# A hybrid attention and RG-LRU block on one Trainium2 core: weights packed in order of use, squares and sums of the inputs on other engines

## The chip, the cores and the metric

The kernel runs on 1 core of a Trainium2 chip. The metric is device time of one launch in microseconds (us). Three runs of the kernel before gave 1709.41, 1717.29 and 1715.06 us, median 1715.06. The engines are TensorE (PE; PEld is its weight loads), VectorE (DVE), ScalarE (ACT), GpSimd (POOL) and SyncE (SP), which here issues nearly all DMAs. A buffer in SBUF has 128 partitions (P).

## The reference

One layer, 256 tokens of width 2048, memory of 256 tokens, all in 32-bit floats:

```
h = rmsnorm(x, g_mix);  proj = h @ w_in        # q, k, v, forget, LRU x, LRU gate, memory q, merge gates
y_fox = forgetting_attention(q, k, v, log_f)   # 8 heads of 128
y_lru = rg_lru(conv4(lx)) * gelu(lg)           # width 1024
mk, mv = split(rmsnorm(mem, g_mem) @ w_mem_kv)
y_mem = memory_attention(qm, km, vm)           # 4 heads of 256
merged = sum(sigmoid(gate_logits + b_gate) * (branches @ w_branch))
x = x + merged @ w_out
up = conv3(rmsnorm(x, g_ffn) @ w_ffn_up);  x = x + (gelu(u_act) * u_val) @ w_ffn_down
```

`rmsnorm(x, g)` is `x * rsqrt(mean(x*x) + eps) * g`, the mean over the 2048 channels.

## The kernel before

All weights, 568 units of 512 x 256 floats (512 KB), stream through four slots. Channels lie on partitions and tokens along the free dimension; x and mem are each 16 tiles (kt) of 128 channels by 256 tokens. For precision each operand is held as a high part (rounded to fp32r) and the low rest, and three of the four products are computed: one matmul of 512 columns and one of 256, 16 matmuls a unit.

A unit u passes through these steps, all in order on their engines:

- SP `load` (L315 to L321) waits for lo_done of unit u-4 and fills slot u mod 4 of `raw`.
- ScalarE `split` (L585 to L593) waits for the weights and for TensorE to have finished unit u-4 (the wait for pe_units u-3), and copies `raw` to the high part of `W`.
- VectorE `split` (L894 to L898) subtracts, giving the low part, and counts up lo_done.
- TensorE `group` (L345 to L375) waits for lo_done of u and multiplies into `psG`; 4 units make a group, 256 output columns. When a group's last unit is u, ScalarE copies half of the sum (`copy_low`, L601) and VectorE adds the other (`add_low`, L904) ahead of their split of u+4.

Units 0 to 15 are phase mv (memory values, from XM = gained mem), 16 to 19 memory keys (XM), 20 to 23 memory queries (the first that read X, the normed and gained x), and so on. The root of mem is not in XM: it is applied later, to k by GpSimd (`scale_k`, L1360, when unit 19's group has been evacuated, about VectorE's unit 23) and to v by `rstd_tok`.

The start, in order of each engine:

- SP: all parameters (`par`, L325), then four times a mv unit and a chunk of four mem tiles (L328), then four times a chunk of x (L330) and a unit, then constants and `ff_raw` (L335), which takes 16 x 128 pieces of 32 bytes out of w_in.
- ScalarE: four times split(c) and four XM high tiles (`gained_hi`, L723); VectorE: four times split(c) and four XM low tiles (`gained_lo`, L1066). TensorE waits in its first group for every tile (memX_lo).
- From unit 4 on `run_units` calls split(u) and then `start_steps(u)` on ScalarE and on VectorE: parameters at 4, ff_w at 10, the lambda steps at 11 to 13, at unit 16 the roots and reciprocals (L718, L1119), at 18 to 21 the X high and low tiles of chunks 0 to 3.
- GpSimd (L1329 to L1353): squares of mem chunk by chunk, added up and folded to `sum1`, then the same of x; after the reciprocal, x_n = x * rstd in four products of 128x1024.
- TensorE adds over partitions by a matmul with ones (`channel_sums`, both inputs at once and the per-token column), as a hook after unit 12.

In the weight arrays a unit is 512 rows of 1 KB, each in its own row of w_in (49184 bytes apart), w_mem_kv and so on. xT and memT are 2048 rows of 1 KB.

Of the kernel before, what the change touches and what calls it, by code (L numbers as in the profile page):

```python
# [12 lines left out]
P = 128  # L34
# [43 lines left out]
for _name, _n in [("g_mix", KT), ("g_mem", KT), ("g_ffn", KT), ("b_gate", 3 * KT), ("w_fconv", 3 * 2 * FT),  # L78
                  ("b_fconv", 2 * FT), ("w_lconv", 4 * BT), ("b_lconv", BT), ("b_a", BT), ("b_x", BT),
                  ("lam", BT), ("g_q", 1), ("g_k", 1), ("g_qm", 2), ("g_km", 2), ("b_f", 1)]:  # L80
    PAR[_name] = _c
    _c += _n
# [54 lines left out]
def hybrid_layer_kernel(nc, xT, memT, par, shapes_const, w_in, w_mem_kv, w_rg, w_branch, w_out, w_up, w_down, outT):  # L137
    with ExitStack() as ctx:
# [22 lines left out]
        sq0 = sb("sq0", [P, UK, T], 112 * KB)  # L161
        sum0 = sb("sum0", [P, 2, UK, T], 116 * KB)
        sum1 = sb("sum1", [P, 2, T], 124 * KB)
# [82 lines left out]
        par_in, const_in, ff_in, rg_in = sem("par_in"), sem("const_in"), sem("ff_in"), sem("rg_in")  # L246
        setup, ones_set, pool_step = sem("setup"), sem("ones_set"), sem("pool_step")
        act_warm = sem("act_warm")
        sq_done, ss_done, rstd_done = sem("sq_done"), sem("ss_done"), sem("rstd_done")
# [26 lines left out]
        rows = lambda w: w.rearrange("(k p) c -> p k c", p=P)  # L276
        w_in_r, w_kv_r, w_br_r, w_out_r, w_up_r, w_down_r = map(rows, (w_in, w_mem_kv, w_branch, w_out, w_up, w_down))

        def unit_source(phase, i, k, q):

            if phase == "down":
                w, kk = k // (FT // UK), k % (FT // UK)
                return w_down_r[:, kk * UK:(kk + 1) * UK, bass.ds(i * (4 * UC) + w * UC, UC)]
            if phase == "branch0":
                return w_br_r[:, bass.ds(i * BT + (k % 2) * UK, UK), bass.ds(q * (2 * UC) + (k // 2) * UC, UC)]
            w, kk = k // 4, k % 4
            if phase == "gate0":
                src, col = w_in_r, i * D + q * (2 * UC) + (COL_GATE + w * UC)
            elif phase == "mv":
                src, col = w_kv_r, i * (2 * UC) + (BW + w * UC)  # L290
            elif phase == "mkq":
                src, col = (w_kv_r, i * UC) if w == 0 else (w_in_r, i * UC + COL_MQ)
            elif phase == "lru":
                src, col = w_in_r, i * UC + (COL_LX if w == 0 else COL_LG)
            elif phase == "v":
                src, col = w_in_r, i * (2 * UC) + (COL_V + w * UC)
            elif phase == "qk":
                src, col = w_in_r, i * UC + (COL_Q if w == 0 else COL_K)
            elif phase == "out":
                src, col = w_out_r, i * (2 * UC) + w * UC  # L300
            else:
                src, col = w_up_r, i * UC + w * FFN
            return src[:, kk * UK:(kk + 1) * UK, bass.ds(col, UC)]


# [9 lines left out]
        def _(sp):  # L315
            def load(phase, i, k, u, coef, before=0, q=0):

                s = u % SLOTS
                if i is not None or u >= SLOTS:
                    sp.wait_ge(lo_done, at(u - 3, i, coef) + before)  # L320
                sp.dma_start(raw[:, s], unit_source(phase, 0 if i is None else i, k, q)).then_inc(raw_full[s], 16)  # L321

            mem_r = memT.rearrange("(k p) t -> p k t", p=P)
            x_r = xT.rearrange("(k p) t -> p k t", p=P)
# [10 lines left out]
            sp.dma_start(ff_raw[:], w_in_r[:, :, COL_FF:COL_FF + 8]).then_inc(ff_in, 16)  # L335
            def load_phase(name, first=0, before=0, q=0):
                n, per = next((n, per) for ph, n, per in PHASES if ph == name)
                with sp.Fori(first, n) as i:
                    for k in range(NG[name] * per):
                        load(name, i, k, U0[name] + k, NG[name] * per, before, q)  # L340

            load_phase("mv", first=1)
            for name in ("mkq", "lru", "v", "qk"):
                load_phase(name)
            with sp.Fori(0, 4) as q:  # L345
                load_phase("gate0", before=q * QUARTER_UNITS, q=q)
                load_phase("branch0", before=q * QUARTER_UNITS, q=q)
            for name in ("out", "up", "down"):
                load_phase(name)
# [1117 lines left out]
```

## Time and profile before

| | |
|---|---|
| median of three runs | 1715.06 us |
| span of the profiled execution | 1705.0 us |
| TensorE busy, weight loads | 1670.0 us, 1445.4 us |
| VectorE, ScalarE, GpSimd busy | 1136.7, 888.3, 126.4 us |
| DMA | 306.34 MB, mean 180 GB/s, 307168 of 308044 packets under 2 KB |

A row of the order of time reads: start in us, duration in us, engine, line, operation, output <- inputs, shape, count; in brackets the idle time before it and what ended it. Rows of instructions by line give counts and durations in ns (min/median/max), first and last start in us. Rows by stretch give for each engine busy us and the count of instructions, then the granted TensorE clock (1.00 is 2.4 GHz, 0.50 is 1.2 GHz), the mean busy share of the DMA engines and GB/s. Busy time of TensorE is modelled at its ends; a change of the clock is known only from the first one on.

### The profile page before, as it was taken

Reading aid. Unit: us, or ns where it says so; the run is one execution under the profiler, and the core shown is the slowest. Engines: PE = TensorE matmul, PEld = TensorE weight load, DVE = VectorE, ACT = ScalarE, POOL = GpSimd, SP = SyncE. Lnnn points to the kernel's source line nnn. Section 1 sums busy time; section 2 is a strip of 40 time slices with the busy share of each in tenths; the row PEclk is TensorE's granted clock in tenths of the full one; section 3 lists DMA queues with packets and bytes.
Section 4 is the critical chain, followed back from the end, with each engine's and each line's share of the span. In section 5 each row is a group of like instructions: output and inputs, shape, how many; then the busy total and the mean of one; then the engine's idle time right before and its main releaser. Section 6 shows DMA issues by size and latency. Waiting matters only on the chain.

```text
span 1705.0 us, 27268 instructions
## 1 busy us (share of the span) xinstructions
PE 1670.0 (98%) x9386; PEld 1445.4 (85%) x9386; DVE 1136.7 (67%) x1302; ACT 888.3 (52%) x1135; POOL 126.4 (7%) x90
## 2 busy tenths in 40 slices
PE   4999999999999999999999999999999999999998
PEld 3778888887888888888888888888888888888887
DVE  8786667668765647466576677777777777644543
ACT  3466667555654545544545555555555555433342
POOL 7132212120000000000001000000000000000000
PEclk7899999999999999999999999999999999999999
DMA  6555557564555766657655656666555665666653
GB/s 211 161 161 160 145 157 204 161 173 136 150 155 183 191 185 180 189 183 187 184 186 184 189 168 197 197 188 193 183 186 185 196 192 184 197 204 198 203 191 110
DMA packets 308044, 306.34 MB, mean 180 GB/s; under 512 B 11744, under 2 KB 307168, under 8 KB 308000
## 3 DMA queue, kind: packets, MB, share of 16 engines
q1 hardware_dynamic: 307056, 302.89, 58.4%
q0 software_dynamic: 944, 2.88, 0.6%
q8 instruction: 25, 0.41, 0.1%
q14 instruction: 19, 0.16, 0.0%
HBM read 303.64 MB, written 2.10 MB: 179 GB/s over the span
## 4 chain that ended last, share of the span: by engine, by line
PE 95%; DVE 3%; DMA 1%; ACT 0%; POOL 0%; issue 0%; SPq 0%; ACTq 0%; DVEq 0%; POOLq 0%
PE psG L360 91%; PE psM L360 3%; DVE XM L1066 1%; DVE W L898 1%; DMA mem_raw<-memT 0%; DVE X L1066 0%; DMA lru_rg<-w_rg 0%; DVE rstd L1119 0%; POOL x_n L1353 0%; PE psM L448 0%; PE psM L446 0%; ACT X L723 0%; ACT L718 0%; ACT W L593 0%; POOL lru_rg L1386 0%
## 5 line engine op out<-in xcount | busy, mean ns | idle before, releaser
L360 PE MATMUL psG<-X,W 128*128 128x512 f32 (+1 forms) x5632 | 995.4, 338 | 0.0
L360 PEld LDWEIGHTS psG<-X,W 128*128 128x128 f32 x5632 | 862.1, 188 | 125.4 <-issue 3.4
L898 DVE TENSOR_TENSOR W<-raw,W 128x1024 fp32r<-128x1024 f32 x568 | 700.2, 1246 | 334.3 <-ACT W L593 331.8
L593 ACT ACTIVATE W<-raw 128x1024 fp32r<-128x1024 f32 x568 | 592.0, 1054 | 356.1 <-PE psG L360 349.5
L360 PE MATMUL psG<-hidden,W 128*128 128x512 f32 (+1 forms) x1408 | 244.2, 336 | 0.0
L360 PEld LDWEIGHTS psG<-hidden,W 128*128 128x128 f32 x1408 | 215.2, 188 | 28.9
L601 ACT ACTIVATE low<-psG 128x512 f32<-128x512 f32 x140 | 83.7, 598 | 239.1 <-PE psG L360 239.1
L360 PE MATMUL psG<-Y,W 128*128 x768 | 136.3, 340 | 0.0
L360 PEld LDWEIGHTS psG<-Y,W 128*128 128x128 f32 x768 | 117.7, 188 | 18.0
L1259 DVE SCALAR_TENSOR_TENSOR up_c<-up_pad,par_sb,up_c 128x256 f32<-128x256 f32 x176 | 77.5, 482 | 42.4 <-ACT up_c L842 36.4
L360 PE MATMUL psG<-merged,W 128*128 128x512 f32 (+1 forms) x512 | 90.6, 340 | 0.0
L360 PEld LDWEIGHTS psG<-merged,W 128*128 128x128 f32 x512 | 78.4, 188 | 12.1
L360 PE MATMUL psG<-W,XM 128*128 128x512 f32 (+1 forms) x256 | 59.9, 397 | 25.8 <-DVE XM L1066 25.2
L842 ACT ACTIVATE up_c<-up_pad,par_sb 128x256 f32<-128x256 f32 x88 | 48.2, 596 | 60.5 <-DVE up_pad L1251 60.5
L360 PEld LDWEIGHTS psG<-W,XM 128*128 128x128 f32 x256 | 47.2, 227 | 37.8 <-issue 21.5
L904 DVE TENSOR_TENSOR yd<-psG,low 128x512 f32<-128x512 f32 x40 | 27.7, 692 | 51.3 <-ACT low L601 51.3
L1426 POOL DMA_DIRECT2D outT<-xs x7 | 5.1, 734 | 696.7 <-DVE xs L1305 696.7
L360 PE MATMUL psG<-XM,W 128*128 128x512 f32 (+1 forms) x256 | 49.1, 350 | 3.1 <-DVE W L898 3.1
L360 PEld LDWEIGHTS psG<-XM,W 128*128 128x128 f32 x256 | 40.6, 194 | 10.5 <-DVE W L898 3.9
L904 DVE TENSOR_TENSOR up_pad<-psG,low 128x512 f32<-128x512 f32 x44 | 30.4, 692 | 27.7 <-ACT low L601 27.7
L866 ACT ACTIVATE hidden<-up_c 128x512 f32 (+1 forms) x22 | 13.9, 632 | 65.3 <-DVE up_c L1284 65.3
L360 PE MATMUL psG<-W,X 128*128 128x512 f32 (+1 forms) x256 | 45.4, 338 | 0.0
(181 smaller groups left out, 789.8 us busy)
## 6 DMA issues: line engine op xcount, KB each, us to landing
raw<-w_in SPq DMA_DIRECT2D x192, 512.0 KB, 4.1
raw<-w_up SPq DMA_DIRECT2D x176, 512.0 KB, 4.5
raw<-w_down SPq DMA_DIRECT2D x88, 512.0 KB, 3.5
raw<-w_branch SPq DMA_DIRECT2D x48, 512.0 KB, 3.4
raw<-w_mem_kv SPq DMA_DIRECT2D x32, 512.0 KB, 3.7
raw<-w_out SPq DMA_DIRECT2D x32, 512.0 KB, 4.2
mem_raw<-memT SPq DMA_DIRECT2D x4, 512.0 KB, 9.1
xs<-xT SPq DMA_DIRECT2D x4, 512.0 KB, 8.6
```

The source lines that it names most:

```text
L360: return nc.tensor.matmul(*a, skip_group_check=True, **kw)
L593: nc.scalar.activation(W[:, s, :, 0], raw[:, s], ACT.Copy).then_inc(hi_done, 1)
L601: nc.scalar.activation(low[:, g % 2], psG[:, b:b + 2, T:], ACT.Copy).then_inc(low_copied, 1)
L842: ins = nc.scalar.activation(up_c[w][:, t], up_pad[w][:, t, 2:], ACT.Identity, bias=p1("b_fconv", i * 2 + (w * FT + t)), scale=p1("w_fconv ...
L866: nc.scalar.activation(hidden[:, bass.ds(i * 2, 2), 0, :], up_c[1][:], ACT.Copy).then_inc(hidden_hi, 1)
L898: V.tensor_tensor(W[:, s, :, 1], raw[:, s], f32(W[:, s, :, 0]), ALU.subtract).then_inc(lo_done, 1)
L904: V.tensor_tensor(dst, psG[:, b:b + 2, 0:T], low[:, g % 2], ALU.add).then_inc(evac_done, 1)
L1066: ins = V.scalar_tensor_tensor(dst[:, k, 1, :], src[:, k], p1(gain, k), f32(dst[:, k, 0, :]), ALU.mult, ALU.subtract)
L1259: ins = V.scalar_tensor_tensor(up_c[w][:, t], up_pad[w][:, t, n:n + T], p1("w_fconv", i * 2 + (n * 2 * FT + w * FT + t)), up_c[w][:, t], A ...
L1426: G.dma_start(outT[bass.ds(i * UC, UC), :].rearrange("(a p) t -> p a t", p=P), xs[:, bass.ds(i * 2, 2)]).then_inc(out_stored, 16)
```

## The change

- All weights come as one array `w_units` [568, 128, 1024], the units in their order of use, each partition's 4 KB in one piece; SP's loads from unit 8 on are one loop. xT and memT are stored as [128, 16, 256], so a partition's four tiles of a chunk are 4 KB in one piece. `w_ff` is stored apart, one piece of 512 bytes per partition.
- SP first loads the 16 columns of g_mem (`gain_in`); then mem chunk before weights; the rest of the parameters after the four pairs.
- ScalarE in the first four units does the XM tiles before the split. At units 4 to 7 it squares a chunk of x, at 10 to 13 a chunk of mem.
- VectorE adds the squares: for x at units 6, 8 and 9, for mem at 12, 14 and 15. It makes the reciprocal of x at unit 12, x_n at 13 to 16 and the X low tiles at 16 to 19 (ScalarE the high ones there too). The roots and reciprocals of mem come at unit 22.
- TensorE's hook is in two: `x_sums` after unit 8, `mem_sums` after unit 17.
- GpSimd's start is gone; it begins with `scale_k`.

```diff
-            sp.dma_start(par_sb[:], par).then_inc(par_in, 16)
+            sp.dma_start(par_sb[:, 0:KT], par[:, 0:KT]).then_inc(gain_in, 16)
             for c in range(4):
-                load("mv", None, c, c, 0)
-                sp.dma_start(mem_raw[:, 4 * c:4 * c + 4], mem_r[:, 4 * c:4 * c + 4]).then_inc(mem_in[c], 16)
+                sp.dma_start(mem_raw[:, 4 * c:4 * c + 4], memT[:, 4 * c:4 * c + 4]).then_inc(mem_in[c], 16)
+                load(c, c)
+            sp.dma_start(par_sb[:, KT:], par[:, KT:]).then_inc(par_in, 16)
             for c in range(4):
-                sp.dma_start(xs[:, 4 * c:4 * c + 4], x_r[:, 4 * c:4 * c + 4]).then_inc(x_in[c], 16)
-                load("mv", None, 4 + c, 4 + c, 0)
+                sp.dma_start(xs[:, 4 * c:4 * c + 4], xT[:, 4 * c:4 * c + 4]).then_inc(x_in[c], 16)
+                load(c, 4 + c, c + 1)
...
-            sp.dma_start(ff_raw[:], w_in_r[:, :, COL_FF:COL_FF + 8]).then_inc(ff_in, 16)
...
+            sp.dma_start(ff_raw[:], w_ff).then_inc(ff_in, 16)
+            with sp.Fori(2, U_ALL // SLOTS) as i:
+                for s in range(SLOTS):
+                    sp.wait_ge(lo_done, i * SLOTS + (s - 3))
+                    src = w_units[bass.ds(i * SLOTS + s, 1)].rearrange("a p (k c) -> p (a k) c", k=UK)
+                    sp.dma_start(raw[:, s], src).then_inc(raw_full[s], 16)
...
-            def channel_sums():
-
-                pe.wait_ge(sq_done, 2)
-                mm(psM[:, 0, :], ones[:], sum1.rearrange("p j t -> p (j t)"), start=True, stop=True)
+            def x_sums():
+                pe.wait_ge(sums_ready, 1)
+                mm(psM[:, 0, 0:T], ones[:], sum1[:, 0], start=True, stop=True).then_inc(ss_done, 1)
+
+            def mem_sums():
+                pe.wait_ge(sums_ready, 2)
+                mm(psM[:, 1, 0:T], ones[:], sum1[:, 1], start=True, stop=True)
...
-                    group("mv", i, w, m_op, {4: channel_sums}, rows_major=True)
+                    group("mv", i, w, m_op, {0: x_sums}, rows_major=True)
...
-            mkq(None, {})
+            mkq(None, {1: mem_sums})
...
             for c in range(4):
-                split(c)
                 act.wait_ge(mem_in[c], 16)
                 for k in range(4 * c, 4 * c + 4):
                     gained_hi(XM, mem_raw, "g_mem", (k,)).then_inc(memX_hi, 1)
+                split(c)
+            act.wait_ge(par_in, 16)
 
             def start_steps(u):
+                if 4 <= u < 8:
+                    act.wait_ge(x_in[u - 4], 16)
+                    nc.scalar.activation(sq0[:, u - 4], xs[:, 4 * (u - 4):4 * (u - 4) + 4], ACT.Square).then_inc(sq_done, 1)
+                if 10 <= u < 14:
+                    act.wait_ge(sum_step, 4)
+                    act.wait_ge(sums_ready, 1)
+                    nc.scalar.activation(sq0[:, u - 10], mem_raw[:, 4 * (u - 10):4 * (u - 10) + 4], ACT.Square).then_inc(sq_done, 1)
...
-                if u == 16:
+                if u == 12:
                     act.wait_ge(ss_done, 1)
-                    root_mean_square(rstd0.rearrange("p j t -> p (j t)"), psM[:, 0, :])
-                    root_mean_square(rstd_tok[:], psM[:, 1, 0:2]).then_inc(root_done, 1)
-                if 18 <= u < 22:
-                    c = u - 18
+                    root_mean_square(rstd0[:, 1], psM[:, 0, 0:T]).then_inc(root_done, 1)
+                if u == 22:
+                    act.wait_ge(ss_done, 2)
+                    root_mean_square(rstd0[:, 0], psM[:, 1, 0:T])
+                    root_mean_square(rstd_tok[:], psM[:, 2, 0:2]).then_inc(root_done, 1)
+                if 16 <= u < 20:
+                    c = u - 16
...
+                for first, j in ((6, 0), (12, 1)):
+                    if u == first:
+                        dve.wait_ge(sq_done, 4 * j + 2)
+                        V.tensor_tensor(sq0[:, 0], sq0[:, 0], sq0[:, 1], ALU.add).then_inc(sum_step, 1)
+                    if u == first + 2:
+                        dve.wait_ge(sq_done, 4 * j + 4)
+                        V.tensor_tensor(sq0[:, 2], sq0[:, 2], sq0[:, 3], ALU.add).then_inc(sum_step, 1)
+                        dve.wait_ge(sum_step, 4 * j + 2)
+                        V.tensor_tensor(sq0[:, 0], sq0[:, 0], sq0[:, 2], ALU.add).then_inc(sum_step, 1)
+                    if u == first + 3:
+                        dve.wait_ge(sum_step, 4 * j + 3)
+                        V.tensor_tensor(sq0[:, 0, 0:2], sq0[:, 0, 0:2], sq0[:, 0, 2:4], ALU.add).then_inc(sum_step, 1)
+                        dve.wait_ge(sum_step, 4 * j + 4)
+                        V.tensor_tensor(sum1[:, j], sq0[:, 0, 0], sq0[:, 0, 1], ALU.add).then_inc(sums_ready, 1)
...
-                if u == 16:
+                if u == 12:
                     dve.wait_ge(root_done, 1)
-                    V.reciprocal(rstd0[:], rstd0[:])
+                    V.reciprocal(rstd0[:, 1], rstd0[:, 1]).then_inc(rstd_done, 1)
+                if u == 22:
+                    dve.wait_ge(root_done, 2)
+                    V.reciprocal(rstd0[:, 0], rstd0[:, 0])
                     V.reciprocal(rstd_tok[:], rstd_tok[:]).then_inc(rstd_done, 1)
-                if 18 <= u < 22:
-                    c = u - 18
+                if 13 <= u < 17:
+                    c = u - 13
+                    dve.wait_ge(rstd_done, 1)
+                    V.tensor_tensor(x_n[:, 4 * c:4 * c + 4], xs[:, 4 * c:4 * c + 4],
+                                    rstd0[:, 1:2].to_broadcast([P, 4, T]), ALU.mult).then_inc(x_scaled, 1)
+                if 16 <= u < 20:
+                    c = u - 16
                     dve.wait_ge(xX_hi, c + 1)
...
-            pool.wait_ge(rstd_done, 1)
-            for c in range(4):
-                G.tensor_tensor(x_n[:, 4 * c:4 * c + 4], xs[:, 4 * c:4 * c + 4],
-                                rstd0[:, 1:2].to_broadcast([P, 4, T]), ALU.mult).then_inc(x_scaled, 1)
+            pool.wait_ge(rstd_done, 2)
```

## Rows read from the trace of the kernel before

**Rows 1.** The page: busy time of TensorE, and its busy tenths by slice.
```profile
PE 1670.0 (98%) x9386; PEld 1445.4 (85%) x9386; DVE 1136.7 (67%) x1302; ACT 888.3 (52%) x1135; POOL 126.4 (7%) x90
...
PE   4999999999999999999999999999999999999998
```

**Rows 2.** Busy time by stretch: all engines, clock, DMA share, GB/s.
```profile
12.00:49.00 37.00, 22.79 (x65) 15.48 (x65) 37.00 (x20) 10.91 (x19) 35.25 (x17) 0.66 0.51 154
36.00:49.00 13.00, 6.76 (x17) 4.37 (x18) 13.00 (x8) 1.06 (x3) 12.40 (x7) 0.56 0.30 66
80.00:100.00 20.00, 16.93 (x95) 14.50 (x95) 18.68 (x15) 13.40 (x25) 11.76 (x4) 0.97 0.33 84
```

**Rows 3.** Waits, the whole span: who waited for whom, us, times, longest.
```profile
PE psG L360 <- DVE XM L1066: 25.2, 11, 11.6
```

**Rows 4.** Order of time, the first 49 us.
```profile
5.30 1.06 ACT L593 ACTIVATE W<-raw 128x1024 fp32r<-128x1024 f32 x1 [2.94 <-DMA raw<-w_mem_kv]
...
9.18 1.70 ACT L723 ACTIVATE XM<-mem_raw,par_sb 128x256 fp32r<-128x256 f32 x4 [2.83 <-DMA mem_raw<-memT]
...
11.55 5.46 PE L360 MATMUL psG<-W,XM 128*128 128x512 f32 x16 [11.55 <-DVE XM L1066]
...
15.21 1.71 ACT L723 ACTIVATE XM<-mem_raw,par_sb 128x256 fp32r<-128x256 f32 x4 [0.35 <-DMA mem_raw<-memT]
...
18.23 1.71 ACT L723 ACTIVATE XM<-mem_raw,par_sb 128x256 fp32r<-128x256 f32 x4 [0.37 <-DMA mem_raw<-memT]
...
48.81 11.54 PE L360 MATMUL psG<-W,XM 128*128 128x512 f32 x49 [0.57 <-DVE W L898]
```

**Rows 5.** Instructions of L1066 and L898, count and ns min/median/max.
```profile
L1066 DVE SCALAR_TENSOR_TENSOR XM<-mem_raw,par_sb,XM x16: 474/2108/2595, 9.7 to 43.9; 128x256 fp32r<-128x256 f32 x16
L1066 DVE SCALAR_TENSOR_TENSOR X<-x_n,par_sb,X x16: 469/472/2640, 89.0 to 104.6; 128x256 fp32r<-128x256 f32 x16
...
L898 DVE TENSOR_TENSOR W<-raw,W x568: 1153/1225/3386, 6.4 to 1690.3; 128x1024 fp32r<-128x1024 f32 x190
```

**Rows 6.** Order of time, 60 to 106 us.
```profile
62.45 0.49 DVE L1093 TENSOR_TENSOR ff_w<-ff_raw,ff_w 128x128 fp32r<-128x128 f32 x2
...
66.10 0.17 DVE L1102 SCALAR_TENSOR_TENSOR lam_d<-lam_u,lam_m 128x8 f32<-128x8 f32 x1
...
66.94 1.28 ACT L749 ACT_TABLE_LOAD   x1
...
80.41 3.35 DVE L1119 RECIPROCAL rstd<-rstd 128x512 f32<-128x512 f32 x1 [0.93 <-ACT rstd_tok L718]
...
83.87 11.76 POOL L1353 TENSOR_TENSOR x_n<-xs,rstd 128x1024 f32<-128x1024 f32 x4 [34.53 <-DVE rstd_tok L1120]
...
96.22 0.68 DVE L904 TENSOR_TENSOR mem_v<-psG,low 128x512 f32<-128x512 f32 x1
...
97.96 1.66 DVE L1066 SCALAR_TENSOR_TENSOR X<-x_n,par_sb,X 128x256 fp32r<-128x256 f32 x4
...
98.09 4.62 PE L360 MATMUL psG<-XM,W 128*128 128x512 f32 x16 [3.06 <-DVE W L898]
...
102.55 11.26 PE L360 MATMUL psG<-X,W 128*128 128x512 f32 x64
```

**Rows 7.** DMA of 0 to 50 us: GB/s in 40 slices.
```profile
GB/s 0 61 354 320 301 317 342 386 353 347 349 347 350 350 347 348 348 320 91 34 0 0 0 239 350 243 7 0 0 0 29 317 242 84 10 4 0 0 0 25
```

**Rows 8.** TensorE in two stretches of 60 us: busy, clock, DMA share, GB/s.
```profile
500.00:560.00 60.00, 60.00 (x342) 1.00 0.61 181
980.00:1040.00 60.00, 60.00 (x349) 1.00 0.59 185
```

**Rows 9.** Three windows of 2 us, all engines, clock, DMA share, GB/s.
```profile
12.00:14.00 2.00, 2.00 (x7) 1.65 (x7) 2.00 (x3) 1.80 (x5) 1.75 (x1) 1.00 1.10 348
56.00:58.00 2.00, 2.00 (x13) 1.77 (x12) 0.71 (x1) 0.62 (x1) 0.00 (x0) 1.00 0.76 253
100.00:102.00 2.00, 2.00 (x8) 1.71 (x7) 2.00 (x5) 0.00 (x0) 0.00 (x0) 0.50 0.66 226
```

More of the change, by code:

```diff
@@ L134, in at, with hybrid_layer_kernel @@
     return const if i is None else i * coef + const
[L137 removed]
+def hybrid_layer_kernel(nc, xT, memT, par, shapes_const, w_units, w_ff, w_rg, outT):
     with ExitStack() as ctx:
@@ L274, in f32 @@
             return ap.bitcast(F32)
[L276 to L303, printed above, removed]
         QUARTER0, QUARTER_UNITS = U0["gate0"], U0["gate1"] - U0["gate0"]
@@ L334, in _ @@
             sp.dma_start(mask[:], shapes_const[:, P:P + CW]).then_inc(const_in, 16)
-            sp.dma_start(ff_raw[:], w_in_r[:, :, COL_FF:COL_FF + 8]).then_inc(ff_in, 16)
[L336 to L349, printed above, removed]
+            sp.dma_start(ff_raw[:], w_ff).then_inc(ff_in, 16)
[3 more added lines that the diff above has]
+                    src = w_units[bass.ds(i * SLOTS + s, 1)].rearrange("a p (k c) -> p (a k) c", k=UK)
+                    sp.dma_start(raw[:, s], src).then_inc(raw_full[s], 16)
             for t in (KT - 2, KT - 1):
@@ L1427, in _, with _unit, _unit_sources, _tokens_last @@
             pool.wait_ge(out_stored, 16 * (KT // 2 - 1))
+def _unit(w, sources):
+    src, row, col = sources
+    rows = w[src][row:row + UK * P, col:col + UC]
+    return rows.reshape(UK, P, UC).transpose(1, 0, 2).reshape(P, UK * UC)
+def _unit_sources():
+    for phase, i, w, last in GROUPS:
+        per = next(per for name, _, per in PHASES if name == phase)
+        q = int(phase[-1]) if phase[:-1] in ("gate", "branch") else 0
+        for k in range(per):
+            row = k * UK * P
+            if phase == "down":
+                yield "w_down", row, i * 4 * UC + w * UC
+            elif phase[:-1] == "branch":
+                yield "w_branch", i * BW + row, q * 2 * UC + w * UC
+            elif phase[:-1] == "gate":
+                yield "w_in", row, COL_GATE + i * D + q * 2 * UC + w * UC
+            elif phase == "mv":
+                yield "w_mem_kv", row, BW + i * 2 * UC + w * UC
+            elif phase == "mkq":
+                yield ("w_mem_kv", row, i * UC) if w == 0 else ("w_in", row, COL_MQ + i * UC)
+            elif phase == "lru":
+                yield "w_in", row, (COL_LX if w == 0 else COL_LG) + i * UC
+            elif phase == "v":
+                yield "w_in", row, COL_V + i * 2 * UC + w * UC
+            elif phase == "qk":
+                yield "w_in", row, (COL_Q if w == 0 else COL_K) + i * UC
+            elif phase == "out":
+                yield "w_out", row, i * 2 * UC + w * UC
+            else:
+                yield "w_up", row, i * UC + w * FFN
+def _tokens_last(x):
+    return np.ascontiguousarray(x.T.reshape(KT, P, T).transpose(1, 0, 2))
 def _columns(v):
```

64 lines of the change are left out of this document (22 added, 42 removed).

## The prediction

> **What bounds the kernel now.** I read the page first: TensorE is busy in 98% of the span, and its slice line shows 9 everywhere except in the first tenths [rows 1]. So only what shortens TensorE's idle or half-speed time can shorten the whole, and I went on to the table by stage. It shows where that time lies: from 12 to 49 us TensorE is busy 22.8 of 37 us at a mean granted clock of 0.66; a second, small hole lies at 80 to 100 us, 3.1 us of idle time [rows 2]. In the same 37 us VectorE is busy without a break and so, nearly, is GpSimd (35.25 us), while the DMA share has fallen to 0.30 by the end. The waits name whom TensorE waits for: 25.2 us for VectorE's XM [rows 3].
>
> The order of time shows the pace. First matmul at 11.55, first matmul of unit 4 at 48.81 [rows 4]: 37.26 us for four units. At full clock four units take 11.26 us (2.82 each), and the first unit took 5.46 [rows 4, 6]: it ran at 1.2 GHz, for 12 to 14 us hold 7 matmuls, like the 8 of a stretch granted 0.50 and unlike the 13 at 1.00; the clock column only shows no change there [rows 9]. VectorE is late because its instructions are stretched. An XM tile takes 474 ns at best and 2108 at the median, and the same instruction on X 472 at the median; a split W takes 1225 at the median and 3386 at worst [rows 5]. Four X tiles alone take 1.66 us, four XM tiles at the median 8.4 [rows 5, 6]. The long ones lie where GpSimd runs a tensor_tensor; that is the cause I take. ScalarE and the DMAs are not late: ScalarE's XM had been started by 18.23 at the latest, 30 us before unit 4 [rows 4].
>
> **The change part by part.** All is summed against the profiled span, 1705.0 us; the shown median, 1715.06, is 10.1 above it, and I carry that over.
>
> Squares and sums leave GpSimd. GpSimd then has nothing to do before unit 23. VectorE's work per early unit becomes 1.23 (split) + 1.66 (four XM) = 2.89 us, ScalarE's 1.70 + 1.05 = 2.75, TensorE's 2.82 warm; the loads of one mem chunk and one unit came every 3.02 us (18.23 - 15.21, ScalarE idle on the DMA before each) [rows 4 to 6]. So DMA sets the pace of units 0 to 3, if it stays as it is.
>
> Order of the loads. The 260 KB of parameters no longer stand ahead, only 8 KB of gains. Before, 0.79 MB in order had landed at 5.30 and 1.31 MB at 9.18 [rows 4]; the first chunk and unit, 1.05 MB, then land at about 7.2. ScalarE's split (1.05), VectorE's split (1.23) and one tile (0.47) give a first matmul at about 10.0. Unit 0 runs at half clock (5.46), so TensorE enters unit 4 at 10.0 + 5.46 + 3 x 2.82 = 23.9. Unit 4's weights must cross five pairs and the parameters: about 7.2 + 4 x 3.02 + 0.8 = 20.1, split by 22.4 to 23. They hide under TensorE. Units 5 to 7, each behind an x chunk (SP's queue is in order, and each load waits for a split four units back, early enough), land at 3.02 us intervals. TensorE starts unit 8 at about 36, nearly level with the DMA. On SP the former 2048-piece load of the forget weights becomes 128 pieces; it hides.
>
> Packing. The weight transfers go from pieces of 1 KB to 4 KB. No row shows 4 KB pieces. Bounds: no gain, 348 GB/s, which is what the queue reached under back-pressure; or up to 386, its best [rows 7]. Taken: between, near 370, worth some 2 us at unit 8: pairs every 2.84 us put unit 7 at 7.2 + 7 x 2.84 + 0.7 = 27.8, and the 0.33 MB of constants and unit 8 follow by 30.5, with the lag of a landing. Later it is worth nothing: 181 to 185 GB/s suffice while TensorE has no gap [rows 8]. The Trainium skill, "DMA: Bandwidth & Descriptors", Specifications, wants at least 512 B for line rate, which makes packing worth nothing; its section SWDGE vs HWDGE vs iDMA gives 408.7 GB/s for one core's load stream with 4 KB rows. No run here shows the latter. By the first, unit 20 starts some 2 us later than below, by the second some 2 us earlier.
>
> Added work, units 4 to 22. Four Squares of x on ScalarE at units 4 to 7, about 1.05 each like a Copy of that shape: 2.1 us a unit, under 2.82, hidden. VectorE is where it piles up. From split 8 to split 20 its queue holds: 13 splits x 1.22 = 15.9; of the 128x1024 adds five, 6.2 (a sixth lies in unit 6), each as long as a split; two half and two quarter adds, 2.1; reciprocal of x, half of 3.35 = 1.7; four x_n products, 4.9 (they cost GpSimd 11.76 together); sixteen X tiles, 6.6; three evacuations x 0.68; 0.5 for ff_w and 1.8 for the ten lambda steps of 0.17. Sum 41.7 [rows 5, 6]. Waits for ScalarE come on top: at unit 12 it has a split, a Square, a table load with Ln and a second table load with Sqrt (2 x 1.28, 2.1 for split and Square, about 0.6 for the two small activations: 5.3), and VectorE stands at root_done meanwhile, with the split of unit 13 and the X work behind it; and at unit 9 to 11 the Squares of mem wait for VectorE's last x add. About 3 us together. VectorE starts split 8 at about 31.6 (weights landed 30.5, ScalarE 1.05). So split 20 ends, and unit 20 can start, at 31.6 + 41.7 + 3 = 76.3. TensorE would be there at 36 + 12 x 2.82 + 1.5, allowed for the two sums, = 71.3: it loses about 5 us in units 15 to 17. One clock fall is likely in there: before, 3.06 us of idle time was followed by 0.50, and the unit of 98.09 took until 102.55, 4.46 us instead of 2.82, so 1.6 lost [rows 6, 9]; part of it VectorE's lateness hides. I add 1.2: unit 20 at 77.5.
>
> The tensor waits. x_sums now stands after unit 8 and waits for VectorE's step at unit 9; the next weights are queued behind it. VectorE reaches it at about 37.6 against the unit's end at 38.9, cover 1.3 us; with 3.02 us pairs it would come 1.9 late. mem_sums after unit 17 has over 5 us of cover. The two sums are the matmuls of channel_sums, cut in two; the kernel before had them too, so they cancel. Moving the mem root to unit 22 costs ScalarE 0.7 and VectorE 1.8, under cover: scale_k needs it at unit 23.
>
> Sum: unit 20 (first matmul that reads X) started at 102.55 [rows 6]. 102.55 - 77.5 = 25.0 saved. Span 1705.0 - 25.0 = 1680.0; median 1715.1 - 25.0 = 1690.1. After unit 20 all instructions are the same, so all but this start is carried over.
>
> **The rivals.** (A) The stretch at VectorE's limit doesn't bite: weights early, waits short, TensorE never idles more than a moment: unit 20 at 71 to 73, 30 to 31 saved, 1684. For it: VectorE's chain starts as soon as weights land. Against: 41.7 us of work for 12 units of 2.82.
>
> (B) The limit bites harder: pairs stay at 3.02, x_sums comes late, the clock falls twice or more, and units run at 5.46 when TensorE is also behind. Unit 20 at 81 to 84, 19 to 21 saved, 1695. For it: in the half-idle stretches from 36 us on the clock was 0.56 [rows 2].
>
> (C) TensorE's own rate in the long stretches changes. With no idle time and the same granted clock, 60 us hold 342 matmuls in one stretch and 349 in another [rows 8], 2%, and no row tells why. If the weights' arrival was behind it, and the slow stretches (about 500 us) go to the faster rate: 10 us more, 1680. If the fast stretches (about 800) went to the slower: 16 us lost, 1706. I give 0.035 to each.
>
> (D) Slower than before: packing makes loads slow. If all 128 rows of a unit lie in one 512 KB block and this serves below what TensorE eats, 0.524 MB in 2.82 us = 186 GB/s, every unit waits. At 175 GB/s a unit takes 3.0, and 568 x 0.18 = 102 us come on top: about 1790. It decides from 186 GB/s down; the gain of 25 is used up at 183. Against it: pieces of 1 KB already bring 348.
>
> (E) GpSimd was not what stretched VectorE (ScalarE or the DMAs into SBUF would be): XM stays at 2.1 us and nothing is gained at the start; the added work is lost on top: about 1715 to 1725. Against: from 36 to 49 us ScalarE is busy 1.06 us and the DMA share is 0.30, and VectorE is as slow as before, GpSimd being busy 12.4 of 13 us [rows 2].
>
> **How the numbers follow.** Forecast 0.55 (1686 to 1694), A 0.13, B 0.18, C 0.07, D 0.03, E 0.04. The three runs before lie 8 us apart, which blurs each case by some 3 us. Range: from A's and C's fast side, 1679, to B's slow side, 1700; outside it are D, E, half of C and edges of the others, under 2 in 10. A measurement of this kernel tells about 0.5% (8.6 us) from no change: faster needs under 1706.5. Faster 0.91, same 0.04 (C's slow side, a mild E), slower 0.05 (D, E).
>
> **What would show it.** Right: XM tiles near 0.42 us; GpSimd empty until unit 23; first matmul at about 10; unit 4 at about 24; short TensorE waits for VectorE's W between 55 and 68 us, about 5 together; unit 20 at 77.5; the time from there to the end within 2 us of 1602.5. Wrong: XM near 2 us (E); TensorE waiting for x_sums by over 1 us or several spells at 0.5 (B); other matmul counts per 60 us (C); TensorE idle on raw after unit 24 (D).

## The result, and the profile after

| | before | after |
|---|---|---|
| median of five runs | 1717.29 us (1709.41 to 1719.70) | 1689.76 us (1676.68 to 1690.79) |
| span of the profiled execution | 1705.0 us | 1675.0 us |
| first matmul that reads X (unit 20) | 102.55 us | 72.45 us |
| from there to the end | 1602.45 us | 1602.55 us |

The ratio of the runs is 0.984, with a 95% interval of 0.980 to 0.987: less time, by under 2% but clear of the noise, and the median lies where it was forecast. The two profiles say more than that: 30.1 us were saved ahead of unit 20, not the 25.0 forecast, and nothing behind it. (Over all runs, compared group by group below, it is 27.6 to 27.9 us: the profile of before entered unit 20 late for its kind.) The runs of after also fall into groups 13 us apart; that turned out to be a matter of TensorE's rate, and has an experiment of its own below.

The page of after, busy time and slices (answering [rows 1]), and the stretches of [rows 2]:

```profile
PE 1655.3 (99%) x9388; PEld 1437.3 (86%) x9388; DVE 1114.1 (67%) x1317; ACT 895.0 (53%) x1144; POOL 76.0 (5%) x68
PE   7999999999999999999999999999999999999998
```

```profile
12.00:49.00 37.00, 37.00 (x212) 32.40 (x210) 31.09 (x52) 29.79 (x40) 0.00 (x0) 1.00 0.76 282
36.00:49.00 13.00, 13.00 (x77) 11.46 (x75) 10.12 (x19) 12.94 (x19) 0.00 (x0) 1.00 0.49 164
```

From 12 to 49 us TensorE has gone from 65 matmuls to 212, with GpSimd (the last engine) at 0.00 us. VectorE's XM tiles, 2108 ns at the median before [rows 5], take 479 (min/median/max in ns, then first and last start):

```profile
L1018 DVE SCALAR_TENSOR_TENSOR XM<-mem_raw,par_sb,XM x16: 477/479/481, 9.8 to 19.1; 128x256 fp32r<-128x256 f32 x16
```

The waits of the first 85 us, against the 25.2 us of [rows 3]:

```profile
PE psG L298 <- DVE XM L1018: 10.4, 1, 10.4
PE psG L298 <- DVE W L850: 3.0, 3, 1.9
```

Only the first wait, for the first tile, is left of XM. What is new is 3.0 us in three waits for VectorE's W. The order of time shows both, answering [rows 4] and [rows 6]:

```profile
5.96 1.70 ACT L664 ACTIVATE XM<-mem_raw,par_sb 128x256 fp32r<-128x256 f32 x4 [3.61 <-DMA mem_raw<-memT]
9.79 1.66 DVE L1018 SCALAR_TENSOR_TENSOR XM<-mem_raw,par_sb,XM 128x256 fp32r<-128x256 f32 x4
10.41 26.52 PE L298 MATMUL psG<-W,XM 128*128 128x512 f32 x144 [10.41 <-DVE XM L1018]
29.52 1.23 DVE L850 TENSOR_TENSOR W<-raw,W 128x1024 fp32r<-128x1024 f32 x1 [0.70 <-ACT W L534]
34.91 0.42 DVE L1046 TENSOR_TENSOR sum<-sq 128x256 f32<-128x256 f32 x1
36.77 0.59 PE L298 MATMUL psM<-sum,ones 128*128 128x256 f32 x2
55.90 3.09 PE L298 MATMUL psG<-W,XM 128*128 128x512 f32 x16 [1.89 <-DVE W L850]
59.33 3.02 PE L298 MATMUL psG<-XM,W 128*128 128x512 f32 x16 [0.34 <-DVE W L850]
63.09 3.10 PE L298 MATMUL psG<-XM,W 128*128 128x512 f32 x16 [0.75 <-DVE W L850]
72.45 11.26 PE L298 MATMUL psG<-X,W 128*128 128x512 f32 x64
76.50 2.13 POOL L1309 TENSOR_TENSOR mem_k_raw<-mem_k_raw,rstd 128x512 f32<-128x512 f32 x1 [75.93 <-DVE mem_k_raw L856]
```

The 144 matmuls of units 0 to 8 run without a gap; the sum of x stands ready at 35.3 us, 1.4 us before TensorE asks for it at 36.77. GpSimd does its first work at 76.50.

### The profile page after: what moved, and what is told of

It reads as the page before. It is cut to its first block, busy times and chain, and to the rows that moved or that the text cites. A ratio compares the mean times of both kernels' runs of the same rounds, so it can differ in the third digit from the quotient of the medians.

```text
span 1675.0 us, 27276 instructions
## 1 busy us (share of the span) xinstructions
PE 1655.3 (99%) x9388; PEld 1437.3 (86%) x9388; DVE 1114.1 (67%) x1317; ACT 895.0 (53%) x1144; POOL 76.0 (5%) x68
## 4 chain that ended last, share of the span: by engine, by line
PE 96%; DVE 2%; DMA 1%; ACT 1%; issue 0%; POOL 0%; SPq 0%; ACTq 0%; DVEq 0%; POOLq 0%
PE psG L298 92%; PE psM L298 4%; DVE W L850 1%; DMA raw<-w_units 0%; DVE XM L1018 0%; DMA lru_rg<-w_rg 0%; DMA mem_raw<-memT 0%; DVE x_n L1094 0%; ACT W L534 0%; PE psM L386 0%; DVE sq L1041 0%; DVE sq L1039 0%; ACT sq L686 0%; PE psM L384 0%; ACT XM L664 0%
## 5 line engine op out<-in xcount | busy, mean ns | idle before, releaser
L850 DVE TENSOR_TENSOR W<-raw,W 128x1024 fp32r<-128x1024 f32 x568 | 691.5, 1231 | 330.2 <-ACT W L534 327.8
L298 PE MATMUL psG<-W,XM 128*128 128x512 f32 (+1 forms) x256 | 46.6, 343 | 12.3 <-DVE XM L1018 10.4
L298 PEld LDWEIGHTS psG<-W,XM 128*128 128x128 f32 x256 | 40.1, 193 | 18.2 <-DVE W L850 12.6
L298 PEld LDWEIGHTS psG<-W,X 128*128 128x128 f32 x256 | 39.0, 188 | 5.8
```

Source lines behind the costliest of these rows:

```text
L298: return nc.tensor.matmul(*a, skip_group_check=True, **kw)
L850: V.tensor_tensor(W[:, s, :, 1], raw[:, s], f32(W[:, s, :, 0]), ALU.subtract).then_inc(lo_done, 1)
```

## Experiments

All compare the place where unit 20 starts in the profile, because the timed runs also carry the difference in TensorE's rate. The changed kernel, profiled three times, starts unit 20 at 72.45, 73.99 and 72.31 us, so a difference of under 2 us is not taken for an effect. Of the kernel before there is one profile, with unit 20 at 102.55; its timed runs put the usual place some 2 us earlier (see the section on the prediction), so savings read against 102.55 are some 2 us too large.

### The moved squares and sums alone

The kernel before with the new place of squares, sums, roots and x_n, and with the old arrays and order of loads (unit 0's weights, then mem; all parameters first):

```diff
-            pool.wait_ge(rstd_done, 1)
-            for c in range(4):
-                G.tensor_tensor(x_n[:, 4 * c:4 * c + 4], xs[:, 4 * c:4 * c + 4],
+                V.tensor_tensor(x_n[:, 4 * c:4 * c + 4], xs[:, 4 * c:4 * c + 4],
...
+                if 4 <= u < 8:
+                    nc.scalar.activation(sq0[:, u - 4], xs[:, 4 * (u - 4):4 * (u - 4) + 4], ACT.Square).then_inc(sq_done, 1)
```

> The kernel before with the moved squares and sums alone (layout in DRAM and order of loads as before). Theory: this alone gives most of the gain of 30 us: unit 20 at 77 to 81, 21 to 25 us saved. Rival (the parts only give together): unit 20 after 88.

TensorE in this kernel in order of time, with the three waits that it has left behind its first matmul, and unit 20:

```profile
36.00 3.02 PE L339 MATMUL psG<-W,XM 128*128 128x512 f32 x16 [1.10 <-DVE W L891]
40.50 0.70 PE L339 MATMUL psM<-sum,ones 128*128 128x256 f32 x2 [1.48 <-DVE sum L1087]
...
60.99 4.62 PE L339 MATMUL psG<-W,XM 128*128 128x512 f32 x16 [2.17 <-DVE W L891]
...
77.50 1.78 PE L339 MATMUL psG<-X,W 128*128 128x512 f32 x9
```

Of the 30.1 us, 25.05 come from this part alone, though a wait of 2.17 us was followed here by a unit of 4.62 us instead of 2.8 (a clock fall). The times: 1695.07, 1680.70, 1681.46 and 1685.60, median 1683.53, ratio to the kernel before 0.989 (0.985 to 0.992).

### Packing alone, and packing undone

First the kernel before with w_units, w_ff and the packed xT and memT, nothing else:

```diff
-                sp.dma_start(raw[:, s], unit_source(phase, 0 if i is None else i, k, q)).then_inc(raw_full[s], 16)
+                src = w_units[row].rearrange("p (k c) -> p k c", k=UK)
+                sp.dma_start(raw[:, s], src).then_inc(raw_full[s], 16)
```

> The kernel before with the packing alone: GpSimd still squares and sums, order of loads as before. Theory: XM tiles stay at a median near 2.1 us, TensorE enters unit 4 at 46 to 49 and unit 20 at 100 to 103, within 1% of the kernel before. Rival (packing gives most): unit 20 before 90.

XM in this kernel (durations min/median/max in ns, then first and last start), and unit 20:

```profile
L1025 DVE SCALAR_TENSOR_TENSOR XM<-mem_raw,par_sb,XM x16: 471/2109/2581, 8.9 to 45.2; 128x256 fp32r<-128x256 f32 x16
```

```profile
100.86 1.45 PE L319 MATMUL psG<-X,W 128*128 128x512 f32 x5
```

Loads came at up to 410 to 419 GB/s here, and XM was as slow as before. Unit 20 came 1.7 us earlier than in the profile of before, which is no more than that profile is late; ratio 1.002 (0.998 to 1.005). So packing alone gives nothing that shows. Then the changed kernel with the old arrays, the new order kept:

```diff
-                    src = w_units[bass.ds(i * SLOTS + s, 1)].rearrange("a p (k c) -> p (a k) c", k=UK)
-                    sp.dma_start(raw[:, s], src).then_inc(raw_full[s], 16)
+                sp.dma_start(raw[:, s], unit_source(phase, 0 if i is None else i, k, q)).then_inc(raw_full[s], 16)
```

> The changed kernel with the packing undone: weights, x, mem and forget columns lie in DRAM as before (pieces of 1 KB), order of loads and engines as in the change. Theory (GpSimd's absence is what gives, packing only quickens the first 30 us): XM tiles stay at 0.42 to 0.47 us, the first 12 MB come at about 348 GB/s instead of 410, unit 20 starts 3 to 6 us later than in the changed kernel (72.45), at 76 to 79, span 1678 to 1682. Rival (packing is most of the gain, through quieter DMA): XM tiles slow down and unit 20 starts after 90.

The GB/s of the first 50 us in 40 slices, first the changed kernel, then this one, and this one's unit 20:

```profile
GB/s 0 30 213 272 380 387 397 416 397 419 411 423 401 406 413 410 416 413 406 374 372 402 397 282 285 203 344 33 151 269 265 154 98 324 157 249 16 7 46 328
```

```profile
GB/s 0 16 261 348 349 352 321 342 375 354 347 354 357 351 347 347 350 347 347 348 350 341 246 50 230 241 259 279 355 306 342 115 345 145 305 24 270 185 293 89
```

```profile
76.82 1.46 PE L339 MATMUL psG<-X,W 128*128 128x512 f32 x7
```

In pieces of 4 KB the queue holds some 400 to 420 GB/s, in pieces of 1 KB 347 to 357 where it runs level. The chunks of mem and x lie in one block of 512 KB in both layouts and alternate with the weights here, and no slice from 12 to 26 us shows them faster, which speaks for the length of the pieces and not for where they lie. Unit 20 comes 4.4 us later without packing (2.8 to 4.5 against the three profiles of the changed kernel); TensorE waited 1.5 us for the sum of x and 4.0 us for W. Packing is thus worth more with the sums moved than alone, because only then does the arrival of the weights limit anything. Median 1694.12, ratio 0.993 (0.990 to 0.995).

### The order of the loads undone

```diff
-                sp.dma_start(mem_raw[:, 4 * c:4 * c + 4], memT[:, 4 * c:4 * c + 4]).then_inc(mem_in[c], 16)
                 load(c, c)
-            sp.dma_start(par_sb[:, KT:], par[:, KT:]).then_inc(par_in, 16)
+                sp.dma_start(mem_raw[:, 4 * c:4 * c + 4], memT[:, 4 * c:4 * c + 4]).then_inc(mem_in[c], 16)
```

and all parameters stand at the head again, with ScalarE's split ahead of its XM tiles.

> The changed kernel with the order of the first loads undone: all parameters first, weights before each mem chunk, ScalarE splits before the XM tiles. Theory: first matmul 1 to 1.5 us later than 10.41, as 252 KB more stand ahead and mem lands last; unit 20 0 to 1.5 us later than 72.45, since VectorE's chain, not the first matmul, sets it. Rival (the order of loads carries several us, because chunks land together): unit 20 after 76.

TensorE in order of time:

```profile
10.41 2.90 PE L298 MATMUL psG<-W,XM 128*128 128x512 f32 x8 [10.41 <-DVE XM L1018]
...
58.43 4.46 PE L298 MATMUL psG<-W,XM 128*128 128x512 f32 x16 [2.17 <-DVE W L850]
...
75.07 1.10 PE L298 MATMUL psG<-X,W 128*128 128x512 f32 x5
```

The first matmul starts at 10.41, to the hundredth as in the changed kernel. Unit 20 at 75.07 is 1.1 to 2.8 us later, and this execution had one clock fall after a wait of 2.17 us. The changed kernel, run again, had one too, after 2.21 us, its unit took 4.59, and it reached unit 20 at 73.99. So the order is worth about 1 us or nothing, and the first matmul was not 1 to 1.5 us later, as expected. Median 1690.83, ratio 0.990 (0.986 to 0.994).

### GpSimd busy again, with nothing that anybody waits for

If GpSimd's instructions stretched VectorE's, they must do so as well when they compute something useless. Two kernels: the changed one with GpSimd kept busy from 15.8 us on, in the first by products that read two operands in SBUF, in the second by products with a constant.

```diff
+            for n in range(24):
+                if n:
+                    pool.wait_ge(scratch_step, n)
+                G.tensor_tensor(scratch[:], par_sb[:, 0:512], par_sb[:, 0:512], ALU.mult).then_inc(scratch_step, 1)
```

> The changed kernel with 24 products of 128x512 on GpSimd, each with two SBUF inputs (both from the parameters, the result in a spare buffer and read by nobody), from the landing of the parameters on (about 16 us) to 50 us or later. Theory (VectorE's two-input instructions and GpSimd's slow each other): the XM tiles before 16 us stay at 0.48 us, those after go to 1.5 to 2.6 us, splits W to 2 to 3.4 us, unit 20 starts 12 to 25 us later than 72.45, clock falls again. Rival (something else stretched VectorE, ScalarE or DMA): XM tiles all at 0.48, unit 20 within 3 us of 72.45.

The durations of XM and of the scratch work, then the order of time, then TensorE's wait for the sum of x:

```profile
L1019 DVE SCALAR_TENSOR_TENSOR XM<-mem_raw,par_sb,XM x16: 472/479/1258, 9.6 to 23.7; 128x256 fp32r<-128x256 f32 x16
...
L1309 POOL TENSOR_TENSOR scratch<-par_sb x24: 1057/1633/1982, 15.8 to 52.9; 128x512 f32<-128x512 f32 x24
```

```profile
20.18 4.80 DVE L1019 SCALAR_TENSOR_TENSOR XM<-mem_raw,par_sb,XM 128x256 fp32r<-128x256 f32 x4
...
84.23 1.93 PE L299 MATMUL psG<-X,W 128*128 128x512 f32 x10
```

```profile
PE psM L299 <- DVE sum L1047: 4.6, 1, 4.6
```

Until 15.8 us, where GpSimd is idle, XM takes 0.47; four tiles beside GpSimd take 4.80 us, 1.25 each at a step of about 1.2 (1.5 at least was expected), and a split W 2.06. Unit 20 comes 11.8 us later, at 84.23, just under the 12 of the lower bound. GpSimd is the cause: an engine with no consumer stretched VectorE. One profiled run was taken of each of these two, at 1688.38 and 1698.83 us, beside 1716.81 of the kernel before.

```diff
+            for n in range(44):
+                if n:
+                    pool.wait_ge(scratch_step, n)
+                G.tensor_scalar(scratch[:], par_sb[:, 0:512], 2.0, None, ALU.mult).then_inc(scratch_step, 1)
```

> As the run with two inputs, but 44 GpSimd instructions with one SBUF input (tensor_scalar times 2 of 128x512). Theory (GpSimd's use of SBUF as such slows VectorE's two-input instructions): XM tiles after 16 us at 1 to 2.6 us as well, unit 20 over 8 us late. Rival (only two inputs on both sides collide): XM tiles within 10% of 0.48 us, unit 20 within 3 us of 72.45.

The same views of this second kernel:

```profile
L1019 DVE SCALAR_TENSOR_TENSOR XM<-mem_raw,par_sb,XM x16: 472/478/859, 9.7 to 19.7; 128x256 fp32r<-128x256 f32 x16
...
L1309 POOL TENSOR_SCALAR scratch<-par_sb x44: 1488/1496/2531, 15.8 to 92.2; 128x512 f32<-128x512 f32 x44
```

```profile
30.46 1.65 DVE L1040 TENSOR_TENSOR sq<-sq 128x1024 f32<-128x1024 f32 x1
...
68.56 4.48 PE L299 MATMUL psG<-XM,W 128*128 128x512 f32 x16 [1.81 <-DVE W L851]
...
79.58 1.65 PE L299 MATMUL psG<-X,W 128*128 128x512 f32 x8
```

With one operand in SBUF each GpSimd instruction cost VectorE about 0.4 us once (an add 1.65 instead of 1.22, the longest XM 0.86 instead of 0.48), not the rest of the 1.49 us that GpSimd's own instruction lasted: the tile started at 15.91, 0.12 us behind a GpSimd instruction, took 0.83, and the next one, from 16.66 on beside the same instruction, 0.47. Unit 20 came 7.1 us later: between the theory (over 8) and its rival (under 3), so neither held as written. The Trainium skill, "SBUF — State Buffer", section SBUF: two separate sides, says that VectorE with two operands in SBUF and a GpSimd operation that reads SBUF share a pair of ports as a lock, held for the whole instruction, the other engine fully blocked. The first kernel's 1.25 us beside GpSimd instructions of 1.10 agree; in the second the lock, if that is it, was held for a part of each instruction only.

### The kernel before with GpSimd's work in small pieces

In the profile of before a split W on VectorE and an add on GpSimd stand beside each other like this:

```profile
24.31 2.42 POOL L1344 TENSOR_TENSOR sum<-sum,sq 128x1024 f32<-128x1024 f32 x1
24.44 3.38 DVE L898 TENSOR_TENSOR W<-raw,W 128x1024 fp32r<-128x1024 f32 x1
```

GpSimd's ends at 26.73, and the split, 1.22 us when alone, ends 1.09 us after that. If each instruction of VectorE waits for the end of GpSimd's current one, shorter ones on GpSimd must shorten VectorE's, with the same work in the same place. The squares and adds of 128x1024 were cut in four:

```diff
-                    step(G.tensor_tensor(sum0[:, j], sum0[:, j], sq0[:], ALU.add))
+                    for t in range(4):
+                        step(G.tensor_tensor(sum0[:, j, t], sum0[:, j, t], sq0[:, t], ALU.add))
```

> The kernel before with one thing changed: each GpSimd square and add of 128x1024 is cut into four of 128x256, same work, same engine. Theory (the two engines take turns by whole instructions, so a VectorE instruction with two SBUF inputs waits for the end of GpSimd's current one): XM tiles go from 2.11 us to 0.8 to 1.2 us, splits W under 2.2 us, TensorE enters unit 4 at 32 to 38 instead of 48.81, unit 20 at 86 to 92, 1.5 to 0.5% less time than the kernel before. Rival (they share SBUF bandwidth, so the sum of work counts): XM tiles stay at about 2.1 us, unit 4 after 45.

Its XM durations, and TensorE in order of time (units 4, the sums, unit 20):

```profile
L1066 DVE SCALAR_TENSOR_TENSOR XM<-mem_raw,par_sb,XM x16: 485/832/955, 9.7 to 26.1; 128x256 fp32r<-128x256 f32 x16
```

```profile
28.77 2.62 PE L360 MATMUL psG<-W,XM 128*128 128x512 f32 x13 [0.71 <-DVE W L898]
...
68.50 2.08 PE L360 MATMUL psM<-sum,ones 128*128 128x512 f32 x2 [14.02 <-POOL sum L1352]
...
93.03 1.22 PE L360 MATMUL psG<-X,W 128*128 128x512 f32 x6
```

XM fell from 2.11 to 0.83 us at the median, and TensorE entered unit 4 at 28.77 instead of 48.81, earlier than the 32 to 38 expected. Half of the 20 us was given back at once: GpSimd finishes the sums only at 68.4, and channel_sums waited 14.0 us for them, with the next unit's matmuls queued behind it. Unit 20 at 93.03 (86 to 92 expected), 9.5 us earlier than in the profile of before; median 1700.72, ratio 0.997 (0.993 to 1.000), less than the 0.5% expected. The medians mix the groups of the section on TensorE's rate; group by group it is 8 to 9 us. So the stretch follows the length of GpSimd's instructions: XM takes 2.11 beside 1.89 us, 1.25 beside 1.10, 0.83 beside 0.79. (GpSimd's wait in turn: a product with two operands, 1.06 us at best, took 1.90 when it came beside a split W.)

### The sum of mem later

The three waits of after stand where VectorE's queue is fullest. The root of mem is first used by scale_k on GpSimd, and that can wait; here the root is taken at unit 25 instead of 22:

```diff
-            mkq(None, {1: mem_sums})
+            mkq(None, {5: mem_sums})
...
-                if u == 22:
+                if u == 25:
...
-                for first, j in ((6, 0), (12, 1)):
+                for first, j in ((6, 0), (19, 1)):
```

> The changed kernel with the sums of mem later: VectorE's adds at units 19, 21 and 22 in place of 12, 14 and 15, mem_sums after unit 21 in place of 17, the roots and reciprocals of mem at unit 25 in place of 22. Theory (VectorE's queue from unit 8 to 20 is what made TensorE idle 3.0 us in units 15 to 17): that idle time falls under 0.5 us, unit 20 starts at 69 to 70.5, and no new wait of over 0.5 us appears up to unit 28. Rival (ScalarE's chain of table loads is what binds): idle time stays at 2 us or more. By time the gain of 3 us is within what the runs differ.

TensorE in order of time, units 16 to 20:

```profile
57.23 11.47 PE L298 MATMUL psG<-XM,W 128*128 128x512 f32 x64
69.26 2.01 PE L298 MATMUL psG<-X,W 128*128 128x512 f32 x10 [0.56 <-issue]
```

No wait for W is left before unit 20, which starts at 69.26, 3.2 us earlier. The time from there to the end is 1603.0 to 1603.1 us, some 0.5 more than after's 1602.55: the matmuls of mem_sums, 0.8 us, now lie behind that mark. Some 2.5 of the 3.2 us are thus a gain. The times: median 1676.48, ratio 0.980 (0.974 to 0.985). To see whether it beats the changed kernel both were run side by side:

> The kernel with the sums of mem at units 19 to 22 once more, beside the changed kernel on the same chip. Theory: unit 20 at 69 to 70.5 again, TensorE's waits for W in units 12 to 20 under 0.5 us together; against the changed kernel 3 to 4 us less where both have the same rhythms in the long stretches. Rival (the saved idle time comes back in units 21 to 28, where the moved work now lies): from unit 20 to unit 48 it takes 2 us or more longer than the changed kernel.

> The changed kernel beside the one with the late sums. Theory: unit 20 at 72 to 74, idle time for W 2 to 3 us; timed runs near 1676 or near 1690, by the rhythm of the stretch from about 950 us on.

Medians 1679.49 and 1681.38, ratios to the kernel before 0.983 (0.978 to 0.987) and 0.984 (0.979 to 0.988); spans of the profiles 1672.5 and 1679.5, unit 20 at 69.50 and 72.31. The medians can't tell the gain from nothing, because each mixes the groups of the next section. Group by group they can: the ten runs with late sums (1673.9 to 1674.2, 1679.0 to 1679.6, 1687.7 to 1688.6) all lie below all runs of the changed kernel in their group (1675.3, 1680.0 and 1689.5 at the lowest), by some 2 us at the medians.

### Why the runs of one kernel lie 13 us apart

The changed kernel has three groups of runs, in all its comparisons: 1675.3 to 1677.8, 1680.0 to 1681.7 and 1689.5 to 1690.8. In windows of 60 us without idle time and at clock 1.00, TensorE does either 341 to 342 or 348 to 349 matmuls (the counts take in those that overlap a window's ends; from start to start it is 176.7 or 173.3 ns). TensorE alone, at 500 and at 1200 us; first the profile of after, then a second one of the same kernel, then the kernel with the sums moved alone:

```profile
500.00:560.00 60.00, 60.00 (x341) 1.00 0.60 189
1200.00:1260.00 60.00, 60.00 (x349) 1.00 0.53 178
```

```profile
500.00:560.00 60.00, 60.00 (x348) 1.00 0.57 191
1200.00:1260.00 60.00, 60.00 (x342) 1.00 0.56 187
```

```profile
500.00:560.00 60.00, 60.00 (x342) 1.00 0.64 184
1200.00:1260.00 60.00, 60.00 (x341) 1.00 0.59 187
```

The same instructions take the other rate in another execution. From unit 20 to the end it is 1602.1 to 1603.1 us where only the first window is slow, 1607.2 where only the second is, 1615.4 to 1617.6 where both are, and no profile showed both fast. That orders every profile of this study but the one with added matmuls below, with both layouts of the weights. It was tested whether a short foreign matmul lets TensorE draw its rate anew: one of a single column after each group of the phases up and down.

```diff
+                if phase in ("up", "down"):
+                    mm(psM[:, 3, 0:1], ones[:], ones[:, 0:1], start=True, stop=True)
```

> The changed kernel with one matmul of one column into an unused PSUM bank after each of the 52 groups of the up and down stretch (from about 1030 us). So far each long stretch kept one of two TensorE rhythms, 173.3 or 176.7 ns per matmul, from its first matmul to its last, and changes fell on interruptions. Theory (the rhythm is drawn anew at each interruption): both rhythms appear in this stretch, several groups each; the added matmuls cost 5 to 12 us; the timed runs differ by less than the 14 us seen so far. Rival (the rhythm belongs to the execution or the phase): one rhythm throughout.

> The changed kernel once more, to see what of its trace repeats. [...] Theory: from unit 20 on, the time is 1602 us in the combination slow then fast of the two rhythms, as in the two profiles so far, 1615 to 1616 with both stretches slow, 1594 with both fast; the timed runs fall on such levels, 13 us apart.

TensorE by stretches in the kernel with the added matmuls, the first stretch ahead of the phase up, the second in it:

```profile
500.00:560.00 60.00, 60.00 (x341) 1.00 0.57 188
980.00:1040.00 60.00, 60.00 (x346) 1.00 0.56 178
```

It does not alternate. The 346 count the added ones; between those the unit matmuls follow each other at 176.7 ns through all of up and down, the slower rate, which is the rival's one rhythm throughout. From unit 20 to the end it takes 1626.9 us, 11 more than with both stretches at the slower rate, or some 0.2 us for each added matmul. The ten runs lie at 1692.2 (twice) or 1700.6 to 1702.8: all above those of the changed kernel, with only the step of some 9 us left that belongs to the first stretch, so by their times none of them had the quicker rate in the second. The unchanged kernel beside it has 1675.3 to 1677.8 three times and 1689.8 once. What picks the rate stays open.

## Why the prediction was right

The time came out right, and so did what binds; that it came out within 0.4 us is luck, as worked out below.

**What bounds the start.** Right, and shown three ways: GpSimd idle (XM back to 0.48 us), GpSimd busy for nothing (11.8 us given back), and GpSimd in small pieces (XM 0.83). That ScalarE and the DMAs were not late held too.

**First matmul.** Forecast 10.0, measured 10.41. The path was another, though: mem's first chunk let ScalarE start at 5.96, and without packing at 4.97, the order being the same; why is open. The step that gave the new order of loads a value failed: with the old order the first matmul stood at 10.41 as well.

**Units 0 to 8.** Forecast 5.46 us for unit 0 at half clock and then the pace of the DMA, unit 8 at about 36. Measured 34.0, counted along the 144 matmuls. Unit 0 took 4.18 us here: the window below holds 10 matmuls against 7 before [rows 9], the next 2 us hold 14, so TensorE came to full speed at about 13 us.

```profile
12.00:14.00 2.00, 2.00 (x10) 1.72 (x9) 2.00 (x5) 2.00 (x5) 0.00 (x0) 1.00 1.01 411
```

That was luck. The changed kernel profiled again took 4.63 and 4.98 us for unit 0, and 5.09 with the old order of loads, though TensorE stopped between its first matmuls in none of them, nor in the 5.46 us before. What decides it is open.

And the DMA was above its upper bound: the range ended at 386 GB/s, the best that pieces of 1 KB had shown, and 4 KB brought some 400 to 420. The Trainium skill, "DMA: Bandwidth & Descriptors", section SWDGE vs HWDGE vs iDMA, has 408.7 GB/s for this, and the trace agrees; its Specifications, by which 512 B are enough, fall with 347 to 357 GB/s at 1 KB. By the section that held, unit 20 was to come some 2 us earlier than forecast, and the VectorE chain did begin 2.1 us earlier (split 8 at 29.52 instead of 31.6).

**VectorE's queue, units 8 to 20.** The chain was the right one, and its size 44.7 us was 2.5 too long: it ended at about 71.7, 42.2 after its start. Instructions that follow each other overlap by some 0.08 us (adds of 1.22 start 1.14 apart), and durations were added; the wait for the root was 1.89, and those for the Squares were short. TensorE lost 3.0 us in units 15 to 17, in three waits, against 5 forecast in the same units.

**The clock fall.** 1.2 us were set, and after had none; three profiles named above had one after a wait of 2.17 or 2.21 us, and the one with constant products after 1.81 (its unit took 4.48). In after the longest wait was 1.89 us, and its unit took 3.09; and without packing TensorE waited as long as in these three, with no fall:

```profile
60.17 3.05 PE L339 MATMUL psG<-W,XM 128*128 128x512 f32 x16 [2.22 <-DVE W L891]
```

So the length of a wait of this size does not decide it. The sum: 77.5 - 2.1 - 2.5 - 1.2 = 71.7, plus 0.75 for which TensorE itself was late at the end = 72.45. This is rival A's place (71 to 73). A was given 0.13 and not the most, because the shortest waits, the fastest loads and no fall had to come together; the first two share a cause, the quicker loads, which the cases treated as apart, and the third was chance: of three profiles of the changed kernel one had a fall.

**The cover.** x_sums had 1.4 us of cover (1.3 forecast). Without packing it came 1.5 us late (1.9 forecast from pairs every 3.02 us). mem_sums never waited.

**Why the median fits better than the profile.** By luck. The forecast carried over 10.1 us between span and median as if they were overhead. A run takes only 1.6 to 2.0 us more than its span; the rest was the rate of TensorE. In the profile of before it was the quicker pattern, in most of its timed runs a slower one, up to 13 us longer; the same holds for after, where 72.45 + 1615.6 (the rest, in profiles with both stretches at the slower rate) + 1.7 = 1689.75, and the median is 1689.76. Between the profile of after and its median lie 14.8 us, 4.7 more than were carried over, and the forecast start of 77.5 was 5.05 too late: the two errors cancel. With its own 77.5 and the rate that the median had, the forecast would have been 1694.8. And had the median of after fallen into its faster group, the time would have been 1676, under the low end of the range.

The medians differ by 27.5 us where the profiles have 30.1. The runs tell why. The 49 of the kernel before, over all comparisons, lie in three groups as well, at 1701.0 to 1705.9, 1708.6 to 1711.0 and 1715.1 to 1720.5; their medians are 1704.1, 1709.3 and 1717.7, those of the changed kernel's 15 runs 1676.5, 1681.4 and 1689.8. Group by group the change saves 27.6, 27.9 and 27.9 us. The profile of before, with 1705.0 and 1.9 on top, would be later than all 21 runs of its group, so its start of unit 20 is late by some 2 us; why one execution starts later than another was not looked into.

**The rivals.** C saw a real thing, two rates 2% apart, and put it in the wrong place: it changes from run to run, with or without packing. D and E fell, D with some 400 GB/s and more and no wait for W behind the start, E with XM at 0.48.

## What to carry to other kernels

Where VectorE's instructions with two operands in SBUF take several times their best duration, look at what GpSimd runs beside them before counting VectorE's work: moving that work to engines with room was worth five sixths of this change, and cutting it into short instructions helps only until somebody waits for its end. A chain of moved work is to be summed by the distance of starts, not by durations, and with the faster load as one of its bounds. And before a profile is compared with a median, it is worth counting matmuls per equal window, since the profile may show the quicker of two rates. Where the runs of two kernels fall into such groups, compare group with group: a gain of 2 us showed there and in no median.

## What was not expected of the hardware

- TensorE keeps one of two rates, 173.3 or 176.7 ns per matmul at a granted clock of 1.00 and without idle time, through stretches of hundreds of us; 13 us of 1690 between runs of the same kernel.
- A DMA queue with pieces of 4 KB brought some 400 to 420 GB/s, with pieces of 1 KB 347 to 357.
- A GpSimd product of 128x512 with a constant took 1.49 us and held VectorE for about 0.4 of them; one with two operands held it to its end.
- TensorE's first unit, run without a stop, took 4.18, 4.63 and 4.98 us in three profiles of one kernel; and a wait of 2.22 us left it at full clock where one of 1.81 in another kernel did not.
